# Four direct pairs instead of six in each FFN, with the halves' differences formed by VectorE

## The chip, the cores and the metric

The kernel runs on one core of a Trainium2 chip. TensorE (PE) multiplies into PSUM banks; VectorE (DVE), ScalarE (ACT) and GpSimd (POOL) prepare operands and take results; SyncE (SP) issues the loads. The metric is the device time of one execution in microseconds (us), as the median of several runs.

## The reference

One encoder layer on `x` of 512 positions by 1024 channels, all in float32:

```python
x = x + 0.5 * swiglu(rms(x, g_ffn1), w_up1, w_down1)      # FFN 1, D_FF = 2816
h = rms(x, g_mix)
... windowed attention and Fourier mixing, gated ...
x = x + 0.5 * swiglu(rms(x, g_ffn2), w_up2, w_down2)      # FFN 2
out = rms(x, g_final)

def swiglu(h, w_up, w_down):
    gate, up = jnp.split(h @ w_up, 2, axis=-1)
    return (silu(gate) * up) @ w_down
```

The change touches the two products `h @ w_up` (1024 x 5632 weights each) and what is prepared for them.

## The kernel before

**Precision.** Every factor is held as two parts, a rounded one (`_hi`, written by ScalarE as a copy to fp32r) and the rest (`_lo`, original minus rounded, written by VectorE). A product takes three passes over its tiles: hi x hi, hi x lo, and, once the weights' rest is there, lo x hi.

**Up projection.** The 2816 columns of gate and of up are 22 tiles of 128, and a *pair* is one gate tile and one up tile. `DIRECT = 6` pairs go the plain way: a pair is two granules, and a granule is 8 tiles x 3 passes = 24 matmuls of 512 columns. Its sums are scaled by `rstd` afterwards (`gate`, `up` on VectorE), `silu` runs on ScalarE, and `swish` is their product. The other `PAIRS = 16` go through a scheme of the Winograd kind (`pair_frame`): the 2x2 block product of (two halves of the channels) x (two halves of the positions) is made with 7 block products instead of 8, each of 4 tiles x 3 passes = 12 matmuls of 256 columns. It needs sums and differences of the activations' quarters (`t_sum`, 8 blocks of 128x1024: four are written by `normed_h`, four are differences of them, named T_1, T_2, T_4 and T_3), of which 7 are rounded (`t_rounded`) and split (`t_rest`) once per FFN. It also needs sums of the weights' quarters for each pair: two by VectorE (`sums`, which reads `raw` or `raw_b` in place), two by GpSimd (called s2 and s4 below, for the semaphores they raise).

**Order.** Each engine runs a list written by hand, and semaphores join them. While TensorE runs the direct granules, the others prepare what the first frame needs; `direct_pairs` holds the lists of ScalarE and of VectorE. GpSimd makes the four differences there and then two operations for each pair. In a frame TensorE runs product G0 (two block products, named by the weight group), the last product of the frame before, then G1 and G2 (two each). Ahead of the frame's last block product stands

```python
pe.wait_ge(u2_ready, PAIRS * r + q + 1 + 2 * it)
```

and `u2` on VectorE, the first step of its own `pair_frame`, adds the frame's first two products: it comes in VectorE's list behind the whole of `direct_pairs`. The weights of a direct granule are loaded when `split_lo` of four granules before has freed its slot; the first pair's four loads into `raw_b` stand on SP behind the last direct load.

Of the kernel before, what the change touches and what calls it, by code (L numbers as in the profile page):

```python
# [22 lines left out]
ALU = mybir.AluOpType  # L23
# [19 lines left out]
assert sorted(sum(DOWN_TILES, [])) == list(range(FK)) and len(DOWN_PARTS) == SLOTS  # L43


DIRECT = 6
PAIRS = FK - DIRECT
assert DIRECT % 2 == 0 and PAIRS % 2 == 0
UP_GRANULES = 2 * DIRECT + SLOTS * PAIRS
# [45 lines left out]
HK = DK // 2  # L95
# [160 lines left out]
def build(nc, io):  # L256
# [9 lines left out]
    with ExitStack() as ctx:  # L266
# [345 lines left out]
        def _(act):  # L612
# [95 lines left out]
            def direct_hi(r, j):  # L708

                split_hi(G_UP[r] + j)  # L710

            def silu(r, d):

                act.wait_ge(out_read, O_UP[r] + 2 * d + 1)
                nc.scalar.activation(gate_t[d % 2][:, :], gate_t[d % 2][:, :], ACT.Silu).then_inc(silu_ready, 1)

            def direct_pairs(r):

                direct_hi(r, 4)
                direct_hi(r, 5)  # L720
                if r == 1:
                    diagonal_hi(NORM_FFN2)
                silu(r, 0)
                direct_hi(r, 6)
                silu(r, 1)
                direct_hi(r, 7)
                if r == 0:
                    act.wait_ge(row_ready, 1)
                    act.dma_start(bias_rows, bias_row[:, :]).then_inc(bias_stored, 16)
                t_rounded(r, T_B11)  # L730
                direct_hi(r, 8)
                t_rounded(r, T_1)
                t_rounded(r, T_B21)
                direct_hi(r, 9)
                t_rounded(r, T_2)
                silu(r, 2)
                t_rounded(r, T_4)
                direct_hi(r, 10)
                t_rounded(r, T_3)
                t_rounded(r, T_B22)  # L740
                silu(r, 3)
                direct_hi(r, 11)
                group_hi(r, 0, G0)
                silu(r, 4)
                group_hi(r, 0, G1)
                group_hi(r, 0, G2)
                silu(r, 5)

            def t_rounded(r, t):

# [281 lines left out]
        def _(dve):  # L1032
# [94 lines left out]
            def direct_pairs(r):  # L1127

                nrm = NORM_FFN1 if r == 0 else NORM_FFN2
                direct_lo(r, 4)  # L1130
                if r == 1:
                    mean(nrm)
                direct_lo(r, 5)
                if r == 1:
                    diagonal(nrm)
                factors(nrm)
                gate(r, 0)
                up(r, 0)
                gate(r, 1)
                swish(r, 0)  # L1140
                direct_lo(r, 6)
                up(r, 1)
                for i in range(HK):
                    normed_h(nrm, i)
                swish(r, 1)
                direct_lo(r, 7)
                for i in range(HK, DK):
                    normed_h(nrm, i)
                direct_lo(r, 8)
                gate(r, 2)  # L1150
                up(r, 2)
                swish(r, 2)
                t_rest(r, T_B11)
                t_rest(r, T_2)
                direct_lo(r, 9)
                gate(r, 3)
                t_rest(r, T_B21)
                up(r, 3)
                direct_lo(r, 10)
                swish(r, 3)  # L1160
                t_rest(r, T_4)
                t_rest(r, T_1)
                direct_lo(r, 11)
                sums(r, 0)
                gate(r, 4)
                t_rest(r, T_3)
                group_lo(r, 0, G0)
                up(r, 4)
                swish(r, 4)
                t_rest(r, T_B22)  # L1170
                group_lo(r, 0, G1)
                gate(r, 5)
                group_lo(r, 0, G2)
                sums(r, 1)
                up(r, 5)
                swish(r, 5)

            def normed_h(n, m):

                left, right = (T_B11, T_B12) if m < HK else (T_B21, T_B22)  # L1180
                dst = t_sum[:, left:right + 1:right - left, m % HK, :]
                vec.scalar_tensor_tensor(out=dst, in0=halves(tile(xT, m)), scalar=gain(n, m), in1=halves(rstd[:, :]),
                                         op0=ALU.mult, op1=ALU.mult).then_inc(normed, 1)

            def t_rest(r, t):

# [327 lines left out]
        def _(pool):  # L1514
# [8 lines left out]
            for n in range(4):  # L1523

                for m in () if n == NORM_FFN1 else range(1, DK - 1 if n == NORM_FINAL else DK):
                    pool.wait_ge(sq_ready, DK * (n - 1) + m + 1)
                    if m > 1:
                        pool.wait_ge(sum_added, (DK - 1) * (n - 1) + m - 1)
                    nc.gpsimd.tensor_tensor(ssum[:, :], ssum[:, :], sq[:, m % 2, :], ALU.add).then_inc(sum_added, 1)  # L1529
                for i in range(2 if n == NORM_FINAL else 1):  # L1530
                    blocks = slice(2 * i, 2 * i + 2) if n == NORM_FINAL else slice(0, TB)
                    pool.wait_ge(var_ready, n + 1 + i)
                    nc.gpsimd.tensor_tensor(rinv[:, blocks], var[:, blocks], half[:, blocks],
                                            ALU.pow).then_inc(rinv_ready, 1)
                if n in (NORM_FFN1, NORM_FFN2):
                    r = 0 if n == NORM_FFN1 else 1
                    for i, (to, one, two) in enumerate(((T_1, T_B12, T_B11), (T_2, T_B22, T_1), (T_4, T_B21, T_2),
                                                        (T_3, T_B22, T_B12))):
                        pool.wait_ge(normed, 2 * HK * r + (HK if to == T_1 else 2 * HK))
                        if i in (1, 2):  # L1540
                            pool.wait_ge(t_formed, 4 * r + i)
                        nc.gpsimd.tensor_tensor(t_sum[:, to, :, :], t_sum[:, one, :, :], t_sum[:, two, :, :],
                                                ALU.subtract).then_inc(t_formed, 1)
                    for q in range(PAIRS):
                        blk = pair_raw[q % 2]
                        a12, a22 = blk[:, pair_slot(r, G1), 0:HK, :], blk[:, pair_slot(r, G1), HK:DK, :]
                        s2, s3 = blk[:, pair_slot(r, G0), HK:DK, :], blk[:, pair_slot(r, G2), HK:DK, :]
                        pool.wait_ge(s13_ready, 2 * (PAIRS * r + q) + 1)
                        nc.gpsimd.tensor_tensor(s2, a22, s3, ALU.subtract).then_inc(s2_ready, 1)  # L1549
                        pool.wait_ge(s2_ready, PAIRS * r + q + 1)  # L1550
                        nc.gpsimd.tensor_tensor(blk[:, pair_slot(r, G3), 0:HK, :], a12, s2,
                                                ALU.subtract).then_inc(s4_ready, 1)
# [468 lines left out]
```

## Time and profile before

| | |
|---|---|
| median of 3 runs | 988.93 us (988.77 to 989.03) |
| the profiled execution | 989.37 us, of which its span is 987.6 us |
| PE busy | 979.5 us, 99% of the span |
| DVE busy | 681.4 us, 69% |
| ACT busy | 444.6 us, 45% |
| POOL busy | 183.1 us, 19% |
| PE's granted clock, mean | 0.998 of full speed |

The span is what the profiler saw of instructions; 1.8 us of the execution lie around it. A matmul's duration in the trace overlaps the next one's, so PE's pace is read from starts, not from durations. The other engines' durations also run some 0.07 us into the next instruction: what an operation costs in a full queue is the distance of two starts. Times in the rows are from the span's start. FFN 1's up projection runs from 10 us on, FFN 2's from 629 us on.

### The profile page before, as it was taken

The numbers are of one execution on the slowest core, as the hardware profiler recorded it, in microseconds if no ns is written. First come the engines' busy times: TensorE is split into PE (matmuls) and PEld (weight loads), VectorE is DVE, ScalarE is ACT, GpSimd is POOL, SyncE is SP. The second block draws the span as 40 slices with busy tenths as digits, with TensorE's granted clock in tenths as the row PEclk, the third lists the DMA queues.
The fourth block names the chain that finished last, engine by engine and source line by source line (L and its number), as shares of the span: only waits on it lengthen the run. The fifth ranks groups of instructions, "written<-read, shape, count | busy, mean of one in ns | idle before, by whom it ended". The sixth has DMA issues, their size and how long they took to land.

```text
span 987.6 us, 16144 instructions
## 1 busy us (share of the span) xinstructions
PE 979.5 (99%) x5788; PEld 872.9 (88%) x5788; DVE 681.4 (69%) x937; ACT 444.6 (45%) x677; POOL 183.1 (19%) x106
## 2 busy tenths in 40 slices
PE   9999999999999999999999999999999999999997
PEld 8889999999888888888888888888999999988887
DVE  5897989999544346678884564479798989943322
ACT  6534444447323235458773343443354444642322
POOL 1332434330011010000000002242333434000101
PEclk9999999999999999999999999999999999999999
DMA  7513424223433364122123343331333332343222
GB/s 220 166 43 91 123 85 127 86 85 91 133 89 94 110 167 121 55 86 64 44 76 96 106 127 100 93 106 50 101 107 103 109 90 80 106 118 100 83 62 86
DMA packets 188743, 98.26 MB, mean 100 GB/s; under 512 B 13384, under 2 KB 186520, under 8 KB 188704
## 3 DMA queue, kind: packets, MB, share of 16 engines
q1 hardware_dynamic: 186736, 94.40, 32.7%
q10 hardware_dynamic: 1968, 3.35, 0.9%
q8 instruction: 24, 0.39, 0.2%
q14 instruction: 15, 0.12, 0.0%
HBM read 95.61 MB, written 2.11 MB: 99 GB/s over the span
## 4 chain that ended last, share of the span: by engine, by line
PE 98%; issue 1%; DMA 0%; DVE 0%; POOLq 0%; POOL 0%; DVEq 0%
PE bank L1580 19%; PE bank L1581 19%; PE bank L1590 19%; PE bank L1684 11%; PE bank L1680 11%; PE bank L1678 11%; PE bank L1899 1%; PE bank L1800 1%; PE bank L1801 1%; PE bank L1805 1%; PE bank L1585 1%; PE bank L1887 0%; PE bank L1886 0%; PE bank L1917 0%; PE bank L1914 0%
## 5 line engine op out<-in xcount | busy, mean ns | idle before, releaser
L614 ACT ACTIVATE w_hi<-raw 128x1024 fp32r<-128x1024 f32 (+2 forms) x202 | 181.5, 902 | 232.9 <-PE bank L1590 151.6
L1040 DVE TENSOR_TENSOR w_lo<-raw,w_hi 128x1024 fp32r<-128x1024 f32 (+2 forms) x138 | 147.8, 1074 | 137.7 <-ACT w_hi L614 136.0
L1680 PE MATMUL bank<-t_lo,w_hi 128*128 128x256 f32 x896 | 224.7, 283 | 0.0
L1678 PE MATMUL bank<-t_hi,w_hi 128*128 128x256 f32 x896 | 224.6, 283 | 0.0
L1680 PEld LDWEIGHTS bank<-t_lo,w_hi 128*128 128x128 f32 x896 | 172.0, 192 | 0.2
L1678 PEld LDWEIGHTS bank<-t_hi,w_hi 128*128 128x128 f32 x896 | 172.0, 192 | 0.2
L1684 PE MATMUL bank<-t_hi,w_lo 128*128 128x256 f32 x896 | 144.0, 283 | 0.0
L1580 PE MATMUL bank<-a_hi,w_hi 128*128 128x512 f32 (+1 forms) x374 | 140.1, 379 | 0.0
L1581 PE MATMUL bank<-a_lo,w_hi 128*128 128x512 f32 (+1 forms) x374 | 139.4, 377 | 0.0
L1684 PEld LDWEIGHTS bank<-t_hi,w_lo 128*128 128x128 f32 x896 | 123.6, 192 | 0.0
L1529 POOL TENSOR_TENSOR ssum<-ssum,sq 128x512 f32<-128x512 f32 x20 | 30.6, 1528 | 498.9 <-ACT sq L651 498.9
L614 ACT ACTIVATE w_hi<-raw_b 128x1024 fp32r<-128x1024 f32 x64 | 60.8, 949 | 83.3 <-POOL raw_b L1549 40.4
L1208 DVE TENSOR_TENSOR w_lo<-raw,w_hi 128x1024 fp32r<-128x1024 f32 x64 | 90.9, 1420 | 9.3 <-ACT w_hi L614 9.3
L1208 DVE TENSOR_TENSOR w_lo<-raw_b,w_hi 128x1024 fp32r<-128x1024 f32 x64 | 92.7, 1449 | 3.8 <-ACT w_hi L614 3.7
L1590 PE MATMUL bank<-a_hi,w_lo 128*128 128x512 f32 (+1 forms) x374 | 91.2, 377 | 0.0
L1580 PEld LDWEIGHTS bank<-a_hi,w_hi 128*128 128x128 f32 x374 | 70.4, 188 | 12.8
L1581 PEld LDWEIGHTS bank<-a_lo,w_hi 128*128 128x128 f32 x374 | 70.4, 188 | 12.6
L1590 PEld LDWEIGHTS bank<-a_hi,w_lo 128*128 128x128 f32 x374 | 67.8, 188 | 12.8
L1580 PE MATMUL bank<-hf_hi,w_hi 128*128 128x512 f32 x192 | 75.1, 391 | 0.0
L1581 PE MATMUL bank<-hf_lo,w_hi 128*128 128x512 f32 x192 | 74.7, 389 | 0.0
L1580 PE MATMUL bank<-h_hi,w_hi 128*128 128x512 f32 x176 | 69.3, 394 | 0.0
L1581 PE MATMUL bank<-h_lo,w_hi 128*128 128x512 f32 x176 | 68.7, 390 | 0.0
(244 smaller groups left out, 1481.1 us busy)
## 6 DMA issues: line engine op xcount, KB each, us to landing
raw<-in_w_down_dram SPq DMA_DIRECT2D x48, 384.0 KB, 3.0
raw_b<-in_w_up_dram SPq DMA_DIRECT2D x64, 256.0 KB, 3.6
raw<-in_w_up_dram SPq DMA_DIRECT2D x64, 256.0 KB, 3.6
raw<-in_w_up_dram SPq DMA_DIRECT2D x24, 512.0 KB, 3.8
raw<-in_w_in_dram SPq DMA_DIRECT2D x22, 512.0 KB, 3.7
raw<-in_w_down_dram SPq DMA_DIRECT2D x32, 128.0 KB, 2.2
raw<-in_w_out_dram SPq DMA_DIRECT2D x8, 512.0 KB, 3.4
x_rows<-in_x_dram SPq DMA_DIRECT2D x4, 512.0 KB, 6.6
```

The source lines that it names most:

```text
L614: return nc.scalar.activation(dst, src, ACT.Copy, scale=scale)
L1040: vec.tensor_tensor(w_lo[:, s, 0:nk, :], raw[:, s, 0:nk, :], w_hi[:, s, 0:nk, :].bitcast(F32), ALU.subtract).then_inc(w_lo_ready, 1)
L1208: vec.tensor_tensor(w_lo[:, slot, 0:nk, :], pair_raw[q % 2][:, slot, 0:nk, :], w_hi[:, slot, 0:nk, :].bitcast(F32), ALU.subtract).then_inc ...
L1529: nc.gpsimd.tensor_tensor(ssum[:, :], ssum[:, :], sq[:, m % 2, :], ALU.add).then_inc(sum_added, 1)
L1580: nc.tensor.matmul(out_ap, w_hi[:, s, k, :], xh, start=first and i == 0, stop=False)
L1581: mm = nc.tensor.matmul(out_ap, w_hi[:, s, k, :], xl, start=False, stop=False)
L1585: mm = nc.tensor.matmul(out_ap, w_lo[:, s, k, :], xh, start=False, stop=last and i == len(tiles) - 1)
L1590: mm = nc.tensor.matmul(out_ap, w_lo[:, s, k, :], x_parts(k)[0], start=False, stop=last and i == len(tiles) - 1)
L1678: nc.tensor.matmul(out_ap, w_hi[:, slot, at_ + k, :], hi[:, k, :], start=first and k == 0, stop=False, skip_group_check=not first)
L1680: nc.tensor.matmul(out_ap, w_hi[:, slot, at_ + k, :], lo_[:, k, :], start=False, stop=False, skip_group_check=not first)
L1684: mm = nc.tensor.matmul(out_ap, w_lo[:, slot, at_ + k, :], hi[:, k, :], start=False, stop=k == HK - 1, skip_group_check=not first)
L1800: nc.tensor.matmul(o_ap, rows_of(h_hi, k, t), group_of_four(w_hi, slot, kk), start=k == 0, stop=False)
```

## The change

`DIRECT` becomes 4 (so `PAIRS` 18 and `FK` stays 22). The four differences move from GpSimd to VectorE (`t_difference`). VectorE's list takes the four `normed_h` of the first half, the weight sums of pair 0 and the two remaining direct splits earlier. ScalarE's list loses granules 8 to 11 and takes the three weight groups of pair 0 between the `t_rounded`. Nothing changes within `pair_frame`, and no part of the computation is left out.

```diff
-DIRECT = 6
+DIRECT = 4
 ...
@@ ScalarE, direct_pairs, from the split of granule 7 on
                 direct_hi(r, 7)
+                t_rounded(r, T_B11)
                 if r == 0:
                     act.wait_ge(row_ready, 1)
                     act.dma_start(bias_rows, bias_row[:, :]).then_inc(bias_stored, 16)
-                t_rounded(r, T_B11)
-                direct_hi(r, 8)
                 t_rounded(r, T_1)
                 t_rounded(r, T_B21)
-                direct_hi(r, 9)
                 t_rounded(r, T_2)
                 silu(r, 2)
+                group_hi(r, 0, G0)
                 t_rounded(r, T_4)
-                direct_hi(r, 10)
+                group_hi(r, 0, G1)
                 t_rounded(r, T_3)
+                silu(r, 3)
+                group_hi(r, 0, G2)
                 t_rounded(r, T_B22)
-                silu(r, 3)
-                direct_hi(r, 11)
-                group_hi(r, 0, G0)
-                silu(r, 4)
-                group_hi(r, 0, G1)
-                group_hi(r, 0, G2)
-                silu(r, 5)
@@ VectorE, direct_pairs, from gate(r, 1) on
-                swish(r, 0)
-                direct_lo(r, 6)
-                up(r, 1)
                 for i in range(HK):
                     normed_h(nrm, i)
-                swish(r, 1)
+                swish(r, 0)
+                up(r, 1)
+                sums(r, 0)
+                direct_lo(r, 6)
                 direct_lo(r, 7)
+                t_difference(r, 0)
                 for i in range(HK, DK):
                     normed_h(nrm, i)
-                direct_lo(r, 8)
+                t_difference(r, 1)
+                swish(r, 1)
                 gate(r, 2)
+                t_difference(r, 2)
+                t_rest(r, T_B11)
+                t_rest(r, T_2)
+                t_difference(r, 3)
                 up(r, 2)
                 swish(r, 2)
-                t_rest(r, T_B11)
-                t_rest(r, T_2)
-                direct_lo(r, 9)
+                t_rest(r, T_B21)
+                group_lo(r, 0, G0)
                 gate(r, 3)
-                t_rest(r, T_B21)
+                t_rest(r, T_4)
+                group_lo(r, 0, G1)
+                t_rest(r, T_1)
+                sums(r, 1)
                 up(r, 3)
-                direct_lo(r, 10)
+                group_lo(r, 0, G2)
+                t_rest(r, T_3)
                 swish(r, 3)
-                t_rest(r, T_4)
-                t_rest(r, T_1)
-                direct_lo(r, 11)
-                sums(r, 0)
-                gate(r, 4)
-                t_rest(r, T_3)
-                group_lo(r, 0, G0)
-                up(r, 4)
-                swish(r, 4)
                 t_rest(r, T_B22)
-                group_lo(r, 0, G1)
-                gate(r, 5)
-                group_lo(r, 0, G2)
-                sums(r, 1)
-                up(r, 5)
-                swish(r, 5)
@@ VectorE, new
+            def t_difference(r, i):
+                to, one, two = ((T_1, T_B12, T_B11), (T_2, T_B22, T_1), (T_4, T_B21, T_2), (T_3, T_B22, T_B12))[i]
+                dve.wait_ge(normed, 2 * HK * r + (HK if to == T_1 else 2 * HK))
+                if i in (1, 2):
+                    dve.wait_ge(t_formed, 4 * r + i)
+                vec.tensor_tensor(t_sum[:, to, :, :], t_sum[:, one, :, :], t_sum[:, two, :, :],
+                                  ALU.subtract).then_inc(t_formed, 1)
@@ GpSimd: the same loop over the four differences is taken out
```

VectorE's queue in FFN 1 from the read of granule 3's bank on (`ub_t`), before; `w_lo<-raw` is a direct split, `t_sum<-xT` is `normed_h`, L1111 and L1117 are `gate` and `up`, L1124 is `swish`:

```order
L1117 TENSOR_TENSOR ub_t<-bank,rstd 128x512
L1182 SCALAR_TENSOR_TENSOR t_sum<-xT,consts,rstd 128x2x256 x4
L1124 TENSOR_TENSOR a_t<-gb_t,ub_t 128x512
L1040 TENSOR_TENSOR w_lo<-raw,w_hi 128x1024
L1182 SCALAR_TENSOR_TENSOR t_sum<-xT,consts,rstd 128x2x256 x4
L1040 TENSOR_TENSOR w_lo<-raw,w_hi 128x1024
L1111 TENSOR_TENSOR ga_t<-bank,rstd 128x512
```

The same stretch now, in which `raw_b<-raw_b` is `sums` of pair 0 and `t_sum<-t_sum` is `t_difference`:

```order
L1111 TENSOR_TENSOR ub_t<-bank,rstd 128x512
L1195 TENSOR_TENSOR raw_b<-raw_b 128x512
L1196 TENSOR_TENSOR raw_b<-raw_b 128x512
L1034 TENSOR_TENSOR w_lo<-raw,w_hi 128x1024 x2
L1179 TENSOR_TENSOR t_sum<-t_sum 128x1024
L1170 SCALAR_TENSOR_TENSOR t_sum<-xT,consts,rstd 128x2x256 x4
L1179 TENSOR_TENSOR t_sum<-t_sum 128x1024
L1118 TENSOR_TENSOR a_t<-gb_t,ub_t 128x512
L1105 TENSOR_TENSOR ga_t<-bank,rstd 128x512
```

The sums of pair 0 come 17 rows of the queue earlier than before, and the second `swish` and the third `gate` stand behind two of the new differences.

The end of VectorE's list of `direct_pairs` and the first step of `pair_frame` (`u_t<-bank,p_t` is `u2`), before:

```order
L1208 TENSOR_TENSOR w_lo<-raw_b,w_hi 128x1024
L1111 TENSOR_TENSOR gb_t<-bank,rstd 128x512
L1208 TENSOR_TENSOR w_lo<-raw_b,w_hi 128x1024
L1198 TENSOR_TENSOR raw<-raw 128x512
L1199 TENSOR_TENSOR raw<-raw 128x512
L1117 TENSOR_TENSOR ub_t<-bank,rstd 128x512
L1124 TENSOR_TENSOR a_t<-gb_t,ub_t 128x512
L1215 TENSOR_TENSOR u_t<-bank,p_t 128x256
```

The same place now:

```order
L1038 TENSOR_TENSOR t_lo<-t_sum,t_hi 128x1024
L1195 TENSOR_TENSOR raw<-raw 128x512
L1196 TENSOR_TENSOR raw<-raw 128x512
L1111 TENSOR_TENSOR ub_t<-bank,rstd 128x512
L1205 TENSOR_TENSOR w_lo<-raw_b,w_hi 128x1024
L1038 TENSOR_TENSOR t_lo<-t_sum,t_hi 128x1024
L1118 TENSOR_TENSOR a_t<-gb_t,ub_t 128x512
L1038 TENSOR_TENSOR t_lo<-t_sum,t_hi 128x1024
L1212 TENSOR_TENSOR u_t<-bank,p_t 128x256
```

Between the sums of pair 1 and `u2` there are now three operations of 1024 columns (the split of G2 and the rests of T_3 and T_B22) beside an `up` and a `swish`, where there were only an `up` and a `swish`.

## Rows read from the trace of the kernel before

**Rows 1.** The page, busy time and instructions of each engine.
```profile
PE 979.5 (99%) x5788; PEld 872.9 (88%) x5788; DVE 681.4 (69%) x937; ACT 444.6 (45%) x677; POOL 183.1 (19%) x106
```
**Rows 2.** Waits of PE: line, waited for, total us, times, longest.
```profile
PE bank L1639 <- POOL half L1520: 1.7, 1, 1.7
PE bank L1973 <- ACT sq L1016: 0.7, 1, 0.7
```
**Rows 3.** The chain that ended last: start us, us, what.
```profile
76.72 1.81 PE bank L1590 x8
79.49 0.48 PE bank L1684 x4
80.93 0.48 PE bank L1684 x4
...
89.57 0.48 PE bank L1684 x4
```
**Rows 4.** Timeline of PE: start us, us, line, operation.
```profile
56.61 0.39 PE L1580 MATMUL bank<-hf_hi,w_hi 128*128 128x512 f32 x1
...
78.37 0.28 PE L1678 MATMUL bank<-t_hi,w_hi 128*128 128x256 f32 x1
```
**Rows 5.** Timeline of VectorE, the two FFNs' starts and the first u2.
```profile
29.61 0.69 DVE L1074 COPY rstd<-bank 128x512 f32<-128x512 f32 x1
...
81.52 0.42 DVE L1215 TENSOR_TENSOR u_t<-bank,p_t 128x256 f32<-128x256 f32 x1 [1.52 <-PE bank L1684]
...
644.85 0.69 DVE L1074 COPY rstd<-bank 128x512 f32<-128x512 f32 x1 [2.23 <-PE bank L1621]
```
**Rows 6.** Timeline of VectorE between 35 and 45 us.
```profile
35.66 2.73 DVE L1182 SCALAR_TENSOR_TENSOR t_sum<-xT,consts,rstd 128x512 f32<-128x512 f32 x4
38.31 0.68 DVE L1124 TENSOR_TENSOR a_t<-gb_t,ub_t 128x512 f32<-128x512 f32 x1
38.91 1.22 DVE L1040 TENSOR_TENSOR w_lo<-raw,w_hi 128x1024 fp32r<-128x1024 f32 x1
40.05 4.88 DVE L1182 SCALAR_TENSOR_TENSOR t_sum<-xT,consts,rstd 128x512 f32<-128x512 f32 x4
```
**Rows 7.** Timeline of GpSimd.
```profile
38.47 3.92 POOL L1542 TENSOR_TENSOR t_sum<-t_sum 128x1024 f32<-128x1024 f32 x1 [14.85 <-DVE t_sum L1182]
...
65.20 1.69 POOL L1549 TENSOR_TENSOR raw_b<-raw_b 128x512 f32<-128x512 f32 x1 [11.51 <-DVE raw_b L1198]
66.97 2.16 POOL L1551 TENSOR_TENSOR raw_b<-raw_b 128x512 f32<-128x512 f32 x1
...
77.98 1.29 POOL L1551 TENSOR_TENSOR raw<-raw 128x512 f32<-128x512 f32 x1
```
**Rows 8.** Timeline of VectorE beside the first two of these.
```profile
66.25 1.72 DVE L1044 TENSOR_TENSOR t_lo<-t_sum,t_hi 128x1024 fp32r<-128x1024 f32 x1
68.02 2.20 DVE L1208 TENSOR_TENSOR w_lo<-raw_b,w_hi 128x1024 fp32r<-128x1024 f32 x1
...
99.56 2.31 DVE L1208 TENSOR_TENSOR w_lo<-raw_b,w_hi 128x1024 fp32r<-128x1024 f32 x1
101.79 0.41 DVE L1215 TENSOR_TENSOR u_t<-bank,p_t 128x256 f32<-128x256 f32 x1
```
**Rows 9.** Timeline of SP's queue.
```profile
27.48 0.37 SPq L504 DMA_DIRECT2D raw<-in_w_up_dram  x1
...
40.29 0.37 SPq L504 DMA_DIRECT2D raw<-in_w_up_dram  x1
```
**Rows 10.** Stretches: PE, PEld, DVE, ACT, POOL busy; clock, DMA share, GB/s.
```profile
46.50:47.00 0.50, 0.50 (x4) 0.42 (x3) 0.50 (x2) 0.50 (x1) 0.50 (x1) 1.00 0.21 56
...
100.00:120.00 20.00, 20.00 (x169) 20.00 (x168) 18.27 (x23) 9.55 (x14) 7.51 (x5) 1.00 0.36 105
...
984.00:984.50 0.50, 0.00 (x0) 0.00 (x0) 0.00 (x0) 0.00 (x0) 0.00 (x0) 0.61 0.93 352
```
**Rows 11.** Timeline of PE, its last matmuls.
```profile
981.54 0.42 PE L1979 MATMUL bank<-ident,gb_t 128*128 128x128 f32 x2
```

More of the change, by code:

```diff
@@ L1536, in _ @@
                     r = 0 if n == NORM_FFN1 else 1
[L1537 to L1543, printed above, removed]
                     for q in range(PAIRS):
```

## The prediction

> **What bounds the kernel now.** I read the page's busy times first: PE is busy 99% of the span, the next engine 69% [rows 1]. A share that high can still hide a slow feed, so I read the waits of PE next: it waits twice in the whole span, 1.7 us at the start and 0.7 us at the end [rows 2]. Last comes the pace of PE in the chain that ended last: it is even [rows 3]. So TensorE sets the time, nothing that another engine does is late anywhere, and each matmul taken out is worth its full pace, as long as the others still come in time. The question is what happens to their margin in the stretch that the change shortens.
>
> **What TensorE saves.** Granules 8 to 11 take 78.37 - 56.61 = 21.76 us from the first matmul of granule 8 to the first of the first frame [rows 4], so a direct pair takes 10.88 us. A block product takes 80.93 - 79.49 = 1.44 us, and a frame of 7 takes 10.08 us, which is also the distance from 79.49 to 89.57 [rows 3]. A pair moved to the scheme saves 0.80 us, and four of them (two in each FFN) 3.20 us. By this alone the span would be 984.4 us and the median 985.7.
>
> **When the first frame's operands are due now.** TensorE reaches the first frame after granule 7, at 56.61 us, and not at 78.37 [rows 4]. Five block products of that frame stand ahead of its last one (G0, G1 and the first of G2), 5 x 1.44 = 7.20 us, so the last is to start at 63.81. Ahead of it stands the wait for `u2`, which is in VectorE's list behind all of `direct_pairs`. Before, `u2` started at 81.52, as soon as PE had made the products that it reads [rows 5], and it was due at 78.37 + 7.20 = 85.57: VectorE had 3.6 us to spare. Now the same end is due 21.76 us earlier, and I add up what VectorE has to do until then.
>
> **VectorE's chain from `rstd` to `u2`.** It starts at 29.61 [rows 5], which the change doesn't move. Prices are distances of two starts in a full queue: 1.14 for an operation of 1024 columns (38.91 to 40.05), 0.60 for one of 512 (38.31 to 38.91), 0.66 for a `normed_h` (35.66 to 38.31, four of them) [rows 6]. The list is:
> the copy of `rstd`, 0.69;
> 8 reads of `gate` and `up`, 4 `swish` and 4 halves of `sums` (pairs 0 and 1), 16 x 0.60 = 9.60;
> 8 `normed_h`, 5.30;
> 16 operations of 1024 columns, which are 4 differences, 7 rests, the splits of granules 6 and 7 and those of G0, G1 and G2, 16 x 1.14 = 18.24;
> and `u2` itself, 0.41 [rows 8].
> That makes 34.24 us, so `u2` would end at 63.85, and TensorE would lose nothing to speak of. The differences on VectorE have no row of their own: they have the shape and both inputs in SBUF like the split at 38.91, which gives 1.14. Below that I have no bound but the 0.60 of half the columns, and above it the 1.22 that the row's duration says: over four of them -2.2 and +0.3 us.
>
> **What GpSimd adds to it.** An operation of GpSimd that reads SBUF and one of VectorE with both inputs in SBUF don't run side by side. The last of GpSimd's operations of 512 columns, with VectorE idle beside it, took 1.29 us; the two of pair 0 took 1.69 and 2.16 [rows 7], and VectorE's operations beside them 1.72 and 2.20 in place of 1.22 [rows 8], which is 0.50 and 0.98 more. The first was less because VectorE read a PSUM bank in part of that time. In a frame the split beside the same GpSimd operation takes 2.31, 1.09 more [rows 8]. Now both GpSimd operations of pair 0 start when VectorE's sums are made, and VectorE goes on with the splits of granules 6 and 7, all inputs in SBUF: 2 x 1.09 = 2.2 us. The two of pair 1 start at the sums of pair 1; beside the first stands `up(r, 3)`, from a bank, as it did before, so 0.50, and the second meets a rest: 1.09. That is 3.8 us in all, and all of it lies before `u2`. Between ends of 0 (GpSimd always comes last) and 4.4 (no bank read beside any of them) I take 3.8, as the rows of the same meetings show it. Two waits of VectorE on its own last result (the difference after the last `normed_h`, the `swish` after `up(r, 2)`) have no row here: above 0, and I put at most a short instruction's 0.41 on each, with 0.1 as the value.
>
> So `u2` ends at 63.85 + 3.8 + 0.2 = 67.85, and TensorE, due at 63.81, loses 4.0 us there. A first part of it may come earlier, since ScalarE's copy of the first product is queued behind the rounding of T_B22, and both come behind `silu(r, 3)`, which needs VectorE's `gate(r, 3)`; that changes where PE waits, not how long. With the semaphore's way from VectorE to TensorE I take 4.1 us per FFN.
>
> **Is the chain ever idle?** Then it would end later still. Each wait in it is met by my sum. The banks are complete 5.44 us apart, the last at 56.61: granule 3's at 34.85, where VectorE gets to it at 35.4; granule 4's at 40.3 against 47; granule 6's at 51.2 against 56; granule 7's at 56.6 against 61. ScalarE has a round of 1 us for each block and is ahead of each rest by 1 us or more. The loads of pair 0 are what is closest. They stand behind the load of granule 11, issued at 40.29, and the traffic of both dies away in the slice from 46.50 [rows 9, 10], 6.2 to 6.7 us later. Now they stand behind the load of granule 7, issued at 27.48 [rows 9], and are in by 33.7 to 34.2; the sums need them at 36.0. Were they late by 1 us, all behind would be late by 1 us, in both FFNs.
>
> **After the stall.** A stretch of 20 us in the frames holds 18.27 us of VectorE's work [rows 10], so in each frame of 10.08 it has 0.87 us in hand; the splits of G0 and G1 of pair 1 come right behind `u2` and are done before TensorE, set back by the same stall, gets there. So nothing is added, and nothing is made up, for TensorE has no idle time later in which to make it up. The ends of the up projections and all that follows are as they were. In FFN 2 `rstd` is copied at 644.85, 615.24 later than in FFN 1 [rows 5], and the same lists follow, so it costs the same again.
>
> **The sum.** -3.20 + 2 x 4.1 = +5.0 us. The profiled execution had a span of 987.6 and 989.37 us in all; it becomes 992.6 and 994.4. Against the median of 988.93, which lies 0.4 below that execution, it is 993.9 us.
>
> The differences leave GpSimd as well. There they blocked VectorE: the four `normed_h` beside the first took 4.88 in place of 2.73 [rows 6]. The page "Perfetto Trace Analysis" of the Trainium skill, in "Optimizing Scalar/DVE Operations", says that moving work between these two engines might not help, because they share a port of SBUF. The rows agree in this direction too: one difference blocked VectorE for 2.15 us and now costs it 1.14.
>
> **The rivals.**
> *GpSimd gives way (faster).* If GpSimd's operations get in only where VectorE reads a bank or is idle, VectorE's chain stays at 63.85 to 64.3 and each FFN loses 0.5 us at most: -3.2 + 1.0, so 986.7. The point from which this decides is `u2` ending by 63.81 + 1.60 = 65.4, where an FFN breaks even. For it speaks that the split at 38.91 kept its 1.22 although GpSimd's operation had started at 38.47 [rows 6, 7]. Against it speaks that the very next one, at 40.05, was blocked for 2.15: GpSimd was one operation late, not kept out.
> *The chain is half as late.* Prices at their lower ends (differences cheaper, pair 0's two operations blocking once) leave a stall of 1.6 to 2.6 per FFN: 989.0 to 991.
> *The clock falls in the stall.* PE's last matmuls start at 981.54, and in the slice from 984.0 the granted clock is 0.61, so it fell from 2.4 to 1.2 GHz some 2.1 us after the work had ended [rows 10, 11]. A stall of 3.8 us is longer than that, though with dense work right ahead of it, which the end of the kernel has not. If it falls, the matmuls behind the stall run at half pace until it is back; the row of the end shows it down for the 3.4 us from 984.2 to 987.6, and as many after a stall would cost 1.7 us in each FFN: 995.6 with one, 997.3 with both. For it speaks the length, against it that a single wait is all there is.
> The page "TensorE: Matmul & The Clock Gate" of the Trainium skill, in "HAM oscillation — how this bites in real kernels", warns of the same: a gap in TensorE's work that is long enough drops the clock, and the next work starts slow. No stretch of this trace has such a gap between two dense ones.
> *The loads are late.* 1 us or more in both FFNs: 996 and up.
>
> **How the numbers follow.** The forecast of a stall of 3.3 to 4.8 us has 0.58, the clock 0.20, late loads 0.04, the half-late chain 0.09, GpSimd giving way 0.09. The range for 8 in 10 runs from 991.0 to 997.6: below are GpSimd's case and most of the half-late one, above a clock that stays down for longer or late loads. This kernel's runs agree so well that 0.2%, 2 us, is about what can be told from no change: faster means below 986.95, slower above 990.9. Faster gets 0.08; same gets 0.08, the greater part of the half-late case; slower gets 0.84.
>
> **What would show it.** In the waits of PE there are two new ones of 3.5 to 4 us at the last block product of the first frame of each FFN, released by VectorE's `u2`, with a stop at 64 us and, 615.24 later and 2.5 for what FFN 1 lost, at about 681.5. VectorE's timeline is full from 29.6 to 67.8; its splits of granules 6 and 7 take 2.3 each; the sums of pair 0 don't wait. The frame pace is 10.08 before and after. The granted clock stays at 1.00 behind the stall, or it has a slice at half there. I am wrong if PE has no wait at `u2`, or one below 1.6 us, or if it waits for t_hi, t_lo or a weight group first.

## The result and the profile after

The changed kernel takes 997.2 us (median of 4 runs, 996.97 to 997.97) against 988.85 (988.63 to 989.03) for the kernel before in the same session: a ratio of 1.0086, 95% interval 1.0068 to 1.0103. It is slower by 8.4 us. 993.9 had been forecast, with 991.0 to 997.6 as the range. The profiled execution took 997.3 us, its span 995.5, 7.9 more than before.

The page of the changed kernel, busy times (before: [rows 1]) and the engines' shares of the chain that ended last:

```profile
PE 980.2 (98%) x5932; PEld 880.2 (88%) x5932; DVE 704.4 (71%) x969; ACT 452.6 (45%) x693; POOL 181.5 (18%) x106
PE 91%; DVE 6%; issue 2%; DMA 0%; POOLq 0%; POOL 0%; DVEq 0%
```

The same line of the kernel before:

```profile
PE 98%; issue 1%; DMA 0%; DVE 0%; POOLq 0%; POOL 0%; DVEq 0%
```

TensorE's busy time hardly moved while the span grew by 7.9 us, and VectorE is now part of the chain. Where TensorE waited for it stands in the waits of PE (total us, times, longest), which answer to [rows 2]:

```profile
PE bank L1668 <- DVE u_t L1212: 7.1, 2, 3.6
PE bank L1629 <- POOL half L1517: 1.7, 1, 1.7
PE bank L1963 <- ACT sq L1010: 0.7, 1, 0.7
...
```

The two small ones are those of before; the first line is new, and each of its two waits stands at the last block product of a first frame, released by `u2`. In VectorE's timeline of the first one (start, us, operation; to be held against [rows 5, 6]):

```profile
29.60 0.69 DVE L1068 COPY rstd<-bank 128x512 f32<-128x512 f32 x1
...
35.98 0.68 DVE L1195 TENSOR_TENSOR raw_b<-raw_b 128x512 f32<-128x512 f32 x1
...
37.18 2.35 DVE L1034 TENSOR_TENSOR w_lo<-raw,w_hi 128x1024 fp32r<-128x1024 f32 x2
39.45 1.22 DVE L1179 TENSOR_TENSOR t_sum<-t_sum 128x1024 f32<-128x1024 f32 x1
40.59 4.81 DVE L1170 SCALAR_TENSOR_TENSOR t_sum<-xT,consts,rstd 128x512 f32<-128x512 f32 x4
...
61.72 1.72 DVE L1205 TENSOR_TENSOR w_lo<-raw_b,w_hi 128x1024 fp32r<-128x1024 f32 x1
63.36 2.29 DVE L1038 TENSOR_TENSOR t_lo<-t_sum,t_hi 128x1024 fp32r<-128x1024 f32 x1
...
67.32 0.41 DVE L1212 TENSOR_TENSOR u_t<-bank,p_t 128x256 f32<-128x256 f32 x1
```

No row of this stretch, of those left out neither, has an idle time at its end: VectorE works without a break from `rstd` at 29.60, and its `u2` is done at 67.7. GpSimd's timeline beside it (the last column is its own idle time, and what ended it):

```profile
36.74 5.09 POOL L1539 TENSOR_TENSOR raw_b<-raw_b 128x512 f32<-128x512 f32 x1 [13.13 <-DVE raw_b L1195]
41.91 1.62 POOL L1541 TENSOR_TENSOR raw_b<-raw_b 128x512 f32<-128x512 f32 x1
60.68 1.68 POOL L1539 TENSOR_TENSOR raw<-raw 128x512 f32<-128x512 f32 x1 [17.15 <-DVE raw L1195]
...
```

And TensorE's timeline at the stop in FFN 1 and in FFN 2:

```profile
67.78 0.38 PE L1668 MATMUL bank<-t_hi,w_hi 128*128 128x256 f32 x1 [3.56 <-DVE u_t L1212]
68.00 0.28 PE L1670 MATMUL bank<-t_lo,w_hi 128*128 128x256 f32 x1
...
69.65 0.41 PE L1670 MATMUL bank<-t_lo,w_hi 128*128 128x256 f32 x1
...
686.99 0.58 PE L1668 MATMUL bank<-t_hi,w_hi 128*128 128x256 f32 x1 [3.56 <-DVE u_t L1212]
```

The same matmul takes 0.28 us at first and 0.41 from 69.4 on; from start to start it is 0.12 us and then 0.21. Stretches of half a microsecond say why (busy time of PE, PEld, DVE, ACT, POOL, then the granted clock, DMA share and GB/s):

```profile
65.00:65.50 0.50, 0.00 (x0) 0.00 (x0) 0.50 (x1) 0.00 (x0) 0.00 (x0) 1.00 0.00 0
...
68.50:69.00 0.50, 0.50 (x7) 0.50 (x6) 0.50 (x2) 0.00 (x0) 0.00 (x0) 1.00 0.00 0
69.00:69.50 0.50, 0.50 (x6) 0.50 (x5) 0.50 (x2) 0.00 (x0) 0.00 (x0) 0.66 0.00 0
69.50:70.00 0.50, 0.50 (x4) 0.50 (x4) 0.50 (x1) 0.33 (x1) 0.00 (x0) 0.50 0.00 0
...
72.50:73.00 0.50, 0.50 (x6) 0.50 (x6) 0.50 (x2) 0.12 (x1) 0.50 (x1) 0.93 1.07 322
...
687.00:687.50 0.50, 0.50 (x2) 0.50 (x3) 0.50 (x1) 0.00 (x0) 0.00 (x0) 0.50 0.00 0
...
690.00:690.50 0.50, 0.50 (x5) 0.50 (x5) 0.47 (x2) 0.50 (x1) 0.00 (x0) 0.62 0.00 0
```

In FFN 1 the clock is full (2.4 GHz) during the stall and for some 1.4 us of matmuls behind it. Taken from the shares in the first and last slices, it is then at half (1.2 GHz) from about 69.2 to 72.6. In FFN 2 it is at half from 687.0 to 690.4. That is 3.4 us in each. A us at half clock sets these matmuls back by 0.44 us (1 - 0.120/0.213), so 3.4 us cost 1.5.

**The accounting.** The span grew by 7.9 us. The four shorter pairs save 3.20, so 11.1 were lost, 5.55 in each FFN. TensorE was due at 63.81 and went on at 67.78: 3.97 are the stall. The other 1.58 lie behind it: of these, 0.10 is a slow first matmul (67.78 to 68.00), which comes after the wait in the filled kernels below as well, and 1.48 are the slow matmuls of the clock. FFN 2's start bears it out: FFN 1 should be behind by its 5.55 lost less its 1.60 saved, which is 3.95, and this row of VectorE says 648.80 where before it was 644.85 [rows 5]:

```profile
648.80 0.69 DVE L1068 COPY rstd<-bank 128x512 f32<-128x512 f32 x1 [2.23 <-PE bank L1611]
```

In FFN 1 the due time lies 63.81 - 29.61 = 34.20 behind `rstd`. In FFN 2 that is 683.00, and TensorE went on at 686.99, 3.99 late.

### The profile page after: what moved, and what is told of

Its sections match the earlier page's. It is cut to its first block, busy times and chain, and to the rows that moved or that the text cites. A ratio compares the mean times of both kernels' runs of the same rounds, so it can differ in the third digit from the quotient of the medians.

```text
span 995.5 us, 16568 instructions
## 1 busy us (share of the span) xinstructions
PE 980.2 (98%) x5932; PEld 880.2 (88%) x5932; DVE 704.4 (71%) x969; ACT 452.6 (45%) x693; POOL 181.5 (18%) x106
## 4 chain that ended last, share of the span: by engine, by line
PE 91%; DVE 6%; issue 2%; DMA 0%; POOLq 0%; POOL 0%; DVEq 0%
PE bank L1570 16%; PE bank L1571 16%; PE bank L1580 15%; PE bank L1668 12%; PE bank L1670 12%; PE bank L1674 12%; DVE t_lo L1038 2%; DVE t_sum L1170 1%; PE bank L1889 1%; PE bank L1790 1%; PE bank L1791 1%; PE bank L1795 1%; PE bank L1575 1%; PE bank L1877 0%; PE bank L1876 0%
## 5 line engine op out<-in xcount | busy, mean ns | idle before, releaser
L1668 PE MATMUL bank<-t_hi,w_hi 128*128 128x256 f32 x1008 | 255.0, 285 | 7.1 <-DVE u_t L1212 7.1
L1670 PE MATMUL bank<-t_lo,w_hi 128*128 128x256 f32 x1008 | 254.4, 284 | 0.0
L1668 PEld LDWEIGHTS bank<-t_hi,w_hi 128*128 128x128 f32 x1008 | 195.1, 194 | 7.8 <-DVE u_t L1212 7.5
L1670 PEld LDWEIGHTS bank<-t_lo,w_hi 128*128 128x128 f32 x1008 | 195.1, 194 | 0.2
L1674 PE MATMUL bank<-t_hi,w_lo 128*128 128x256 f32 x1008 | 163.2, 284 | 0.0
L1674 PEld LDWEIGHTS bank<-t_hi,w_lo 128*128 128x128 f32 x1008 | 140.0, 193 | 0.2
L1205 DVE TENSOR_TENSOR w_lo<-raw_b,w_hi 128x1024 fp32r<-128x1024 f32 x72 | 103.5, 1438 | 5.0 <-ACT w_hi L614 5.0
L1205 DVE TENSOR_TENSOR w_lo<-raw,w_hi 128x1024 fp32r<-128x1024 f32 x72 | 102.5, 1424 | 6.3 <-ACT w_hi L614 6.3
L614 ACT ACTIVATE w_hi<-raw_b 128x1024 fp32r<-128x1024 f32 x72 | 68.3, 948 | 69.2 <-PE bank L1674 41.1
L1570 PE MATMUL bank<-h_hi,w_hi 128*128 128x512 f32 x176 | 69.2, 393 | 0.0
L1539 POOL TENSOR_TENSOR raw_b<-raw_b 128x512 f32<-128x512 f32 x18 | 36.9, 2053 | 127.2 <-DVE raw_b L1195 127.2
L1539 POOL TENSOR_TENSOR raw<-raw 128x512 f32<-128x512 f32 x18 | 30.1, 1674 | 133.7 <-DVE raw L1195 133.7
```

The lines of the kernel that those rows point to most:

```text
L614: return nc.scalar.activation(dst, src, ACT.Copy, scale=scale)
L1205: vec.tensor_tensor(w_lo[:, slot, 0:nk, :], pair_raw[q % 2][:, slot, 0:nk, :], w_hi[:, slot, 0:nk, :].bitcast(F32), ALU.subtract).then_inc ...
L1570: nc.tensor.matmul(out_ap, w_hi[:, s, k, :], xh, start=first and i == 0, stop=False)
L1668: nc.tensor.matmul(out_ap, w_hi[:, slot, at_ + k, :], hi[:, k, :], start=first and k == 0, stop=False, skip_group_check=not first)
L1670: nc.tensor.matmul(out_ap, w_hi[:, slot, at_ + k, :], lo_[:, k, :], start=False, stop=False, skip_group_check=not first)
L1674: mm = nc.tensor.matmul(out_ap, w_lo[:, slot, at_ + k, :], hi[:, k, :], start=False, stop=k == HK - 1, skip_group_check=not first)
```

## The experiments

The theory: the stall at `u2` costs 4 us in each FFN, it is VectorE's chain that is too long for the shorter start, and the clock that falls costs another 1.5 to 1.6. The rivals: that this remainder is something else (other operands late, slower frames); that GpSimd's blocking has little to do with the length of the chain; that moving the differences is what costs. The kernel before had a median of 988.89 or 988.92 us beside these runs. The profiled executions reach the first `rstd` copy up to 0.7 us apart, so places in them are compared by their distance from the `rstd` copy of their own FFN (29.60 and 648.80 in the changed kernel).

**e1_fill, the stall without its idle time.** The stall stays, but TensorE has something to do in it:

```diff
                 product(r, q, it, G2, 0, T_1, z[:, HALF:SEQ])
+                if q == 0 and isinstance(it, int):
+                    for _ in range(16):
+                        nc.tensor.matmul(banks[W_X[1]][:, :], w_hi[:, pair_slot(r, G2), HK, :], tile(hf_hi, 0), ...)
                 pe.wait_ge(u2_ready, PAIRS * r + q + 1 + 2 * it)
```

> The changed kernel, with 16 more matmuls of 512 columns on TensorE into a bank nobody reads, right ahead of the wait for u2 in the first frame of each FFN (16 x 0.227 = 3.6 us of the 4.0 us stall). Theory: the loss of 5.5 us per FFN is 4.0 us of waiting for VectorE's u2 and 1.5 us of matmuls at half the clock behind the wait. The filled wait ends when u2 does (67.65 us in FFN 1), PE waits 0.3 us at most, the clock stays at 1.00, and the time is 997.2 - 2 x 1.5 = 994.1 us. Rival: there is no cost of the clock, and the missing 1.5 us are later waits of the frames: then the time stays at 997.2 us.

Measured: 994.04 us (ratio 1.0052, 1.0035 to 1.0069). Its `u2` comes as before (37.73 us behind its `rstd` at 29.36, against 37.72), its list of waits has none on it, and its clock is full where the changed kernel's was at half; VectorE's row, and a stretch that answers to the one above:

```profile
67.09 0.41 DVE L1212 TENSOR_TENSOR u_t<-bank,p_t 128x256 f32<-128x256 f32 x1
```
```profile
69.50:70.00 0.50, 0.50 (x6) 0.50 (x6) 0.50 (x1) 0.50 (x1) 0.00 (x0) 1.00 0.00 0
```

Six matmuls instead of four stand in that half microsecond. 997.2 - 994.0 = 3.2 us, 1.6 for each FFN, is the price of the clock by the medians; by the starts of the matmuls it is 1.48, and the difference is within the scatter of the runs. What is left over the kernel before is the stall: -3.20 + 2 x 4.07 = 4.9 us, and 5.1 are measured.

**e6_fill8 and e5_fill4, how much idle time the clock bears.** The same edit with 8 and with 4 matmuls, which leave TensorE idle for a part of the stall.

> The same with 8 filling matmuls (1.8 us): PE idles some 1.8 us. The waits of 1.6 us in the kernel with u2 moved left the clock at 1.00, so I expect no fall and 994.1 us. Rival: idle time in the middle of dense work is counted otherwise, the clock falls for some us, and the time is 995 us or more.

> The changed kernel with 4 filling matmuls of 512 columns (0.9 us) ahead of the wait for u2 in the first frame of each FFN: PE then idles some 2.7 us instead of 3.6. If the fall of the clock needs an idle stretch nearly as long as 3.6 us, it stays at 1.00 and the time is 994.1 us, as with 16; if an idle stretch of 2.7 us is enough, it falls in one FFN or both and the time is 995.6 or 997.2 us.

Measured: 993.87 us with 8 (1.0033 to 1.0065) and 996.92 with 4 (1.0060 to 1.0100). First the wait and a stretch of the kernel with 8, then those of the one with 4:

```profile
PE bank L1668 <- DVE u_t L1212: 3.4, 2, 1.7
```
```profile
69.00:69.50 0.50, 0.50 (x7) 0.50 (x6) 0.50 (x1) 0.50 (x1) 0.00 (x0) 1.00 0.00 0
```
```profile
PE bank L1668 <- DVE u_t L1212: 5.3, 2, 2.6
```
```profile
69.00:69.50 0.50, 0.50 (x4) 0.50 (x4) 0.50 (x2) 0.00 (x0) 0.00 (x0) 0.50 0.00 0
```

With 1.7 us idle in each FFN the clock stays full and the time is that of 16 matmuls. With 2.6 it falls, and the time is that of none. TensorE leaves the stall 38.2 us behind `rstd` in all four kernels and both FFNs, so between the two lies the clock alone: 3.05 us for two falls. The one with 4 has only two runs (996.72 and 997.12), which lie over 2.6 us above all of the other's. Where it falls differs. In FFN 1 of the kernel with 4 it is at about 68.2, after 0.9 us of matmuls; in FFN 2 it is at 686.1, while TensorE is still idle (it goes on at 686.61):

```profile
686.00:686.50 0.50, 0.00 (x0) 0.00 (x0) 0.50 (x3) 0.50 (x1) 0.00 (x0) 0.55 0.00 0
```

**e2_u2_early, the order alone.** `u2` reads only TensorE's first products; here it goes ahead of the three long operations that stood before it.

```diff
                 up(r, 3)
+                u2(r, 0)
                 group_lo(r, 0, G2)
 ...
-                u2(r, q, it)
                 if q:
+                    u2(r, q, it)
                     c12(r, q - 1, it)
```

> The changed kernel with one move: u2 of the first frame stands on VectorE right behind up(r, 3), ahead of the split of G2 and the rests of T_3 and T_B22, in both FFNs. Theory: VectorE's queue as a whole is late, not u2 alone. PE then waits for the rest of T_3 instead, which ends at 65.9 us against 63.8 due (1.8 to 2.1 us), then 0.3 to 0.9 us for the splits and for z behind it, some 3.3 us per FFN with no fall of the clock: 988.85 - 3.2 + 6.6 = 992.3 us. Rival: u2's place alone is the cause, PE waits less than 0.5 us per FFN and the time is 985.7 to 986.6 us.

Measured: 992.29 us (1.0034, 1.0022 to 1.0047), as expected. Its waits of PE:

```profile
PE bank L1669 <- DVE t_lo L1038: 3.1, 2, 1.6
...
PE bank L1669 <- DVE ua_t L1222: 1.3, 2, 0.6
...
PE bank L1675 <- DVE w_lo L1206: 0.3, 2, 0.2
```

The one wait falls apart into three shorter ones: 1.6 us for the rest of T_3, which `u2` was put ahead of, then shorter ones for a split and a read of a bank that stand further down in VectorE's list. VectorE's work did not become less, so this gives back the clock (it is full from 60 to 82 us and at the same place of FFN 2) and part of the stall, not all. It also prices the clock once more: the same 5932 matmuls keep TensorE busy for 977.2 us here and for 980.2 in the changed kernel.

**e3_no_port, GpSimd's share.** GpSimd's two sums of pairs 0 and 1 are replaced by fills with a constant, which read nothing; this leaves those sums out of the computation.

```diff
+                        if q < 2:
+                            nc.gpsimd.memset(s2, 1.0).then_inc(s2_ready, 1)
+                            pool.wait_ge(s2_ready, PAIRS * r + q + 1)
+                            nc.gpsimd.memset(blk[:, pair_slot(r, G3), 0:HK, :], 1.0).then_inc(s4_ready, 1)
+                            continue
                         nc.gpsimd.tensor_tensor(s2, a22, s3, ALU.subtract).then_inc(s2_ready, 1)
```

> The changed kernel, but GpSimd's two weight sums of pairs 0 and 1 in each FFN are replaced by memsets of the same blocks, which read nothing; these sums are left out of the computation. Theory: the four GpSimd operations hold VectorE up for 3.8 us on its way to u2. Then u2 ends at 63.9 us in FFN 1, PE waits 0.3 us or less in each FFN, the clock doesn't fall, and the time is 986.0 to 986.6 us. Rival: GpSimd gives way and costs VectorE little, the chain is long by itself: u2 ends beyond 66 us and the time stays above 992 us.

Measured: 986.79 us (0.9979, 0.9970 to 0.9989), a little above what was expected. `u2` in VectorE's timeline, and the wait for it:

```profile
63.55 0.42 DVE L1212 TENSOR_TENSOR u_t<-bank,p_t 128x256 f32<-128x256 f32 x1
```
```profile
PE bank L1673 <- DVE u_t L1212: 0.4, 2, 0.2
```

`u2` starts 34.05 us behind `rstd` (29.50 here) in place of 37.72, and 34.06 in FFN 2: 3.67 us earlier. That is what GpSimd's four operations cost VectorE, and all but 0.3 us of the stall: TensorE goes on at 64.02, where 34.20 behind `rstd` would be 63.70. The four `normed_h` from 40.48 take their undisturbed time, where the changed kernel's took 4.81:

```profile
40.48 2.74 DVE L1170 SCALAR_TENSOR_TENSOR t_sum<-xT,consts,rstd 128x512 f32<-128x512 f32 x4
```

The time is 2.1 us below the kernel before. Of the 3.2 saved, 2 x 0.3 are this delay and 2 x 0.1 the slow first matmul behind it; 0.3 are left, and the ten runs lie 1.0 apart.

**e7_diff_on_gpsimd, the differences undone.** Four direct pairs in the changed order, but the differences on GpSimd as before.

```diff
-                t_difference(r, 0)   # and (r, 1), (r, 2), (r, 3), where they stood in VectorE's list
@@ GpSimd, ahead of its sums
+                    for i, (to, one, two) in enumerate(((T_1, T_B12, T_B11), (T_2, T_B22, T_1), ...)):
+                        pool.wait_ge(normed, ...)
 ...
+                        nc.gpsimd.tensor_tensor(t_sum[:, to, :, :], t_sum[:, one, :, :], t_sum[:, two, :, :],
+                                                ALU.subtract).then_inc(t_formed, 1)
```

> The changed kernel with one part undone: the four differences of each FFN are formed by GpSimd again, ahead of its weight sums, and taken out of VectorE's list, the rest as it is. Theory: a GpSimd difference holds VectorE's next operation with two SBUF inputs for some 2.2 us and is itself later than VectorE's would be, so VectorE loses more than the 4 x 1.14 us that it is freed of. The first product is late too, u2 still bounds, PE loses some 6.5 us per FFN and 1.5 more where the clock falls: 998.7 to 1001.8 us, slower than the changed kernel. Rival: VectorE is short of time and is freed of 4.5 us, so u2 ends before 65 us, and the time is 987 to 990 us.

Measured: 1003.03 us (1.0140, 1.0123 to 1.0157), 1.2 above the expected range and 5.8 slower than the changed kernel. Its waits of PE, then GpSimd's differences and the rest of VectorE that waited for them:

```profile
PE bank L1671 <- DVE u_t L1208: 7.1, 2, 3.6
PE bank L1671 <- ACT p_t L614: 2.5, 2, 1.3
...
```
```profile
43.58 8.49 POOL L1535 TENSOR_TENSOR t_sum<-t_sum 128x1024 f32<-128x1024 f32 x3 [6.15 <-DVE t_sum L1166]
```
```profile
49.75 3.41 DVE L1038 TENSOR_TENSOR t_lo<-t_sum,t_hi 128x1024 fp32r<-128x1024 f32 x1 [2.30 <-POOL t_sum L1535]
...
69.56 0.41 DVE L1208 TENSOR_TENSOR u_t<-bank,p_t 128x256 f32<-128x256 f32 x1
```

VectorE is freed of 4 x 1.14 us of work, and yet `u2` comes 2.5 us later (40.26 us behind `rstd`, 40.24 in FFN 2, against 37.72): VectorE is idle for 2.30 while it waits for a difference, and a rest takes up to 3.41 beside GpSimd. TensorE loses 6.5 us in each FFN, as expected. The miss is the clock of FFN 1, which is at half from 69.4, while TensorE still waits (it goes on at 70.02), to 76.2:

```profile
69.00:69.50 0.50, 0.00 (x0) 0.00 (x0) 0.50 (x1) 0.50 (x1) 0.00 (x0) 0.89 0.00 0
...
76.00:76.50 0.50, 0.50 (x5) 0.50 (x5) 0.50 (x1) 0.00 (x0) 0.48 (x1) 0.78 0.87 220
```

That is 6.8 us in place of 3.4, with the same listed wait of 3.55 us; the first block products behind it take 2.7 us too long in place of 1.5, which is the 1.2. Ahead of it stand two more waits (0.87 us at 58.3 and 1.26 at 61.7) that the changed kernel has not; whether they matter was not tried. In FFN 2, with the same waits, the clock is down for 3.4 us. So moving the differences is not what costs; with four pairs it is worth 5.8 us, 5.1 by the earlier `u2` and the rest by the clock.

**e8_diff_only, the differences alone.** Six direct pairs and the lists of before, with nothing changed but the four differences, which move from GpSimd to VectorE:

```diff
-DIRECT = 4
+DIRECT = 6
@@ VectorE: the list of before, and in it
                 for i in range(HK):
                     normed_h(nrm, i)
+                t_difference(r, 0)
 ...
                 for i in range(HK, DK):
                     normed_h(nrm, i)
+                for i in range(1, 4):
+                    t_difference(r, i)
@@ GpSimd: the loop over the four differences is taken out
```

> The kernel before with one part of the change alone: six direct pairs, and the four differences on VectorE (the first behind the fourth normed_h, the others behind the eighth). Theory: with six direct pairs VectorE has over 3 us in hand, so PE waits nowhere and the time is 988.9 us, as before. Rival: the differences on VectorE make it late by themselves, and PE waits 0.5 us or more in each FFN: 990 us or more.

Measured: 988.80 us (0.9998, 0.9989 to 1.0008): no difference. There the chain had 3.6 us to spare.

**e4_order, a version that beats both.** If 3.7 us of blocking is what makes the stall, it should pay to let GpSimd's operations start earlier and to put `u2` behind what is due before it and ahead of what is not. The order of VectorE's list (its core), with ScalarE's list to match; nothing else differs but that `c2` of a frame goes from the head of the next frame's list to the end of its own, where it had come in the same sequence:

```diff
+                normed_h(nrm, 0)
+                normed_h(nrm, 1)
+                normed_h(nrm, 2)
+                direct_lo(r, 6)
+                normed_h(nrm, 3)
+                sums(r, 0)
 ...
+                t_rest(r, T_2)
                 t_rest(r, T_B21)
+                sums(r, 1)
+                gate(r, 2)
+                up(r, 2)
 ...
+                up(r, 3)
+                swish(r, 2)
 ...
+                u2(r, 0)
                 group_lo(r, 0, G2)
+                t_rest(r, T_3)
+                group_lo(r, 1, G0)
 ...
+                c2(r, 0)
```

> Four direct pairs as in the changed kernel and the same operations, in another order. VectorE: the sums of pair 0 and 1 and the splits of G0 and G1 earlier, the reads of granules 4 to 7 and their products later, u2 ahead of the rest of T_3, the splits of pair 1's G0 and of G3 ahead of the rest of T_B22, z of frame 0 ahead of the split of pair 1's G1. ScalarE: its groups in the same sequence, silu_c11 of frame 0 last. Theory: what the first frame needs fits ahead of its due times if nothing that it doesn't need stands before it. PE waits nowhere in the two up projections, the clock stays at 1.00, and four pairs save their 3.2 us: 985.7 us (985.3 to 986.5). Rival: VectorE has too much to do in the 27 us between rstd and the first frame in any order; PE still waits 1.5 us or more per FFN and the time is 988.5 us or more.

Measured: 985.64 us over 7 runs (985.34 to 986.02), a ratio of 0.9967 (0.9956 to 0.9978) to the kernel before. Its waits of PE, `u2`, and GpSimd's sums of both pairs:

```profile
PE bank L1640 <- POOL half L1528: 1.7, 1, 1.7
PE bank L1759 <- DMA y_t<-in_b_gate_dram: 0.7, 1, 0.7
...
```
```profile
60.85 0.42 DVE L1225 TENSOR_TENSOR u_t<-bank,p_t 128x256 f32<-128x256 f32 x1
```
```profile
34.92 1.68 POOL L1550 TENSOR_TENSOR raw_b<-raw_b 128x512 f32<-128x512 f32 x1 [11.86 <-DVE raw_b L1208]
...
53.63 1.68 POOL L1550 TENSOR_TENSOR raw<-raw 128x512 f32<-128x512 f32 x1 [14.79 <-DVE raw L1208]
```

No engine is late for TensorE in either FFN: the new 0.7 is a wait for a load elsewhere in the layer, and e8_diff_only, which took no longer than the kernel before, has a like one. `u2` starts 2.4 us before TensorE is due (63.24, as 34.20 behind this run's `rstd` at 29.04). Counted from `rstd`, GpSimd starts 1.3 and 6.5 us earlier, and its operations meet reads of banks (`ga_t`, `ua_t`, `gb_t`, `ub_t`) that now stand behind the sums of either pair. VectorE's rows beside them:

```profile
35.36 0.68 DVE L1115 TENSOR_TENSOR ua_t<-bank,rstd 128x512 f32<-128x512 f32 x1
35.96 1.72 DVE L1038 TENSOR_TENSOR w_lo<-raw,w_hi 128x1024 fp32r<-128x1024 f32 x1
...
54.08 0.67 DVE L1109 TENSOR_TENSOR ga_t<-bank,rstd 128x512 f32<-128x512 f32 x1
```

One split is 0.50 longer than its 1.22, and nothing else is: the port costs 0.5 us in place of 3.7. This and the order of what stands around `u2` came in one kernel, so how much each gave is not told apart. The 988.9 - 985.6 = 3.3 us are what four cheaper pairs are worth.

## Why the prediction was right, and what it left out

**TensorE's saving, 3.20 us: right.** With no stall and no fall of the clock (e4_order) 3.3 us remain, and the accounting closes with 3.20.

**When the operands are due, 63.81: right.** In e3_no_port `u2` ends 34.4 us behind `rstd`, 0.2 behind the due time of 34.2, and TensorE waits 0.2 us for it.

**VectorE's chain, 34.24 and 3.8 for GpSimd: right in sum.** `u2` ended at 67.7; 67.85 had been forecast. Without GpSimd it started 34.05 behind `rstd`, where the sum gives 33.83 and the two waits of VectorE on its own result, put at 0.1 each, the rest; GpSimd's share was 3.67. *Where* pair 0's two operations block was wrong: the splits of granules 6 and 7 were to take 2.3 each, and took 2.35 both together. GpSimd's first operation, released at 36.7, was kept out while VectorE went through the two splits and the difference, and lasted 5.09 us. Both operations were paid for at the `normed_h` from 40.59, with 4.81 in place of 2.73 [rows 6] and of the 2.74 in e3_no_port. That is 2.1 for the 2.2 of the forecast. The hint was in [rows 6, 7]: there too the split at 38.91 kept its 1.22 beside an operation begun at 38.47. The rival *GpSimd gives way* read this as a saving, and it was a delay.

The page "SBUF — State Buffer" of the Trainium skill, in "SBUF: two separate sides", says that the shared port goes for a whole instruction to whichever of the two starts first. The blocked durations agree with this. It would not lead one to expect GpSimd waiting through three instructions of VectorE, and the row of 5.09 us decides.

**The stall, 4.1 us per FFN: right.** It was 3.97 and 3.99, and 0.1 more with the slow first matmul. The list of waits shows 3.56 for each, less than the delay, because it counts from the end of the last matmul.

**The loads of pair 0 in time: right.** The sums at 35.98 follow the read of the bank with no idle time.

**The clock: the term that was left out.** The likeliest case said that the clock stays full, though its own text held the length of the stall against it; the rival *The clock falls in the stall*, at 0.20, gave 1.7 us per FFN and 997.3 for both. Measured were 1.5 to 1.6 per FFN and 997.2. So the mechanism of the stall stood, and the sum lacked a term of 2 x 1.5 = 3.0 us: the span had been forecast at 992.6 and was 995.5. The time lies within the range because the range reaches up to this rival. The step that failed is the weighing. Against the clock stood only that "a single wait is all there is", and e5_fill4 shows that a single wait of 2.6 us in dense work is enough.

That the rival's own size came out so well is luck. It took 3.4 us from the end of the kernel before, but there the span ends with the clock still at half, so the row is only a lower bound for how long it stays down. It could not show that the stay would be the 3.4 us measured in each FFN, and in FFN 1 of e7_diff_on_gpsimd it was 6.8. It also let the matmuls lose half of that time, and they lost 0.44 of it. By its numbers the span would have been 996.0, 0.5 too much; the medians, which have their own scatter, hide this.

The page "TensorE: Matmul & The Clock Gate" of the Trainium skill, in "HAM oscillation — how this bites in real kernels", says that a long enough gap drops the clock and that the next work starts slow, and it counts half of the slow time as lost. FFN 2 agrees with the slow start. In FFN 1 some 1.4 us of matmuls behind the gap still ran at the full clock, and in both the loss is 0.44 of the slow time.

**The frames as before: right.** The chain's pieces behind 72.6 stand 1.44 us apart, as in [rows 3]:

```profile
76.24 0.48 PE bank L1674 x4
...
77.68 0.48 PE bank L1674 x4
```

## What to carry to other kernels

Shortening the stretch in which the other engines prepare the next one moves every due time forward by the whole of what is taken out; add up the helper's list in distances of starts, with what the port adds, against the new due time, before counting the gain. A stall of TensorE as long as these costs the slow matmuls behind it as well, here nearly 40% on top, and eight matmuls that are good for nothing, put into it, took that part back. The order of the helper's list can be worth more than its length, above all what stands in it beside GpSimd's operations: the same operations in another order turned 8.4 us lost into 3.3 gained.

## What the runs showed of the hardware

- The fall of the granted clock need not come while TensorE is idle. In FFN 1 of the changed kernel it was full for some 1.4 us of matmuls after TensorE went on at 67.78. In FFN 2, with the same stall, it was at half from the first matmul on. In FFN 2 of e5_fill4 and FFN 1 of e7_diff_on_gpsimd it fell some 0.6 us before TensorE went on.
- It was at half for 3.4 us in both FFNs of the changed kernel and of e5_fill4 and in FFN 2 of e7_diff_on_gpsimd, and for 6.8 us in FFN 1 of e7_diff_on_gpsimd. A matmul of 256 columns started every 0.21 us at half clock and every 0.12 at full clock, so 3.4 us cost 1.5.
- Idle times of 2.6 and 3.6 us brought one fall each, one of 1.7 us none. Where between 1.7 and 2.6 it turns over was not tried.
- An operation of GpSimd with 512 columns took 5.09 us while VectorE ran three operations of 1024 columns, all with both inputs in SBUF, without a gap. A like one took 1.68 where an `up` from a bank stood beside it. Why it got in at the `normed_h` and not between the three is open: no run separates the kind of operation from the place in the queue.
- A fill with a constant on GpSimd cost VectorE nothing that its rows show (e3_no_port).
